# The transposed copy in a blocked triangular inverse moves from VectorE to TensorE and ScalarE

## The reference

```python
def step(s, inp):
    rt, wt, kt, vt, kkt, bt = inp
    sa = jnp.einsum('bhvk,bhk->bhv', s, kkt)
    s = s * wt[:, :, None, :] - sa[..., None] * bt[:, :, None, :] + vt[..., None] * kt[:, :, None, :]
    return s, jnp.einsum('bhvk,bhk->bhv', s, rt)
```

## Time and profile before

| | |
|---|---|
| median of 3 runs | 3190.02 us (3181.11 to 3193.24) |
| the profiled execution, its time | 3199.97 us |
| its span, first to last instruction | 3198.4 us |
| TensorE busy, matmul | 2887.4 us, 90% |
| VectorE busy | 1812.4 us, 57% |
| ScalarE busy | 1227.5 us, 38% |
| GpSimd busy | 520.2 us, 16% |
| mean granted TensorE clock | 0.951 |
| recurrence of layer 0, first mask to last "done" | 465.01 to 624.28 us |

### The profile page before, as it was taken

The page is one execution under the profiler, slowest core; times in us unless marked ns, Lnnn a source line. Parts: engine busy times, 40 slices in busy tenths (PEclk is TensorE's granted clock), DMA queues, the critical chain, the costliest instruction groups (busy, mean ns, idle before and its releaser), DMA issues. The chain is left out here.

```text
span 3198.4 us, 64194 instructions
## 1 busy us (share of the span) xinstructions
PE 2887.4 (90%) x25830; PEld 2672.7 (84%) x25830; DVE 1812.4 (57%) x2810; ACT 1227.5 (38%) x1637; POOL 520.2 (16%) x341
## 2 busy tenths in 40 slices
PE   7998988889988899899989988987899889998997
PEld 7997877677687898799989978876777878987997
DVE  4444757676666564544344348576765765654442
ACT  4534521044332443444245355210543234434442
POOL 0003640044320000000000046401543100000000
PEclk9999999899999999999989999998999989999998
DMA  4444340144283556344344443401443744663442
GB/s 159 151 143 135 124 126 4 32 122 165 88 307 106 191 205 223 125 144 145 119 140 147 144 133 113 123 4 32 129 172 99 282 161 162 218 216 121 149 147 100
DMA packets 119697, 448.22 MB, mean 140 GB/s; under 512 B 13648, under 2 KB 23920, under 8 KB 111664
## 3 DMA queue, kind: packets, MB, share of 16 engines
q1 hardware_dynamic: 97920, 329.75, 31.4%
q0 software_dynamic: 21552, 115.34, 9.9%
HBM read 397.01 MB, written 48.02 MB: 139 GB/s over the span
## 5 line engine op out<-in xcount | busy, mean ns | idle before, releaser
L1542 ACT ACTIVATE w_high<-ring 128x1024 fp32r<-128x1024 f32 x598 | 632.0, 1057 | 788.6 <-PE gemm_banks L886 331.8
L882 PE MATMUL gemm_banks<-in_high,w_high 128*128 128x320 f32 (+1 forms) x2736 | 810.2, 312 | 24.0 <-DVEq L2263 12.2
L1938 DVE TENSOR_TENSOR w_low<-ring,w_high 128x1024 fp32r<-128x1024 f32 x436 | 532.5, 1222 | 493.5 <-ACT w_high L1542 492.9
L883 PE MATMUL gemm_banks<-in_low,w_high 128*128 128x320 f32 (+1 forms) x2736 | 799.5, 308 | 0.0
L720 POOL TENSOR_TENSOR w_low<-ring,w_high 128x1024 fp32r<-128x1024 f32 x162 | 411.8, 2547 | 927.8 <-ACT w_high L1542 924.0
L882 PEld LDWEIGHTS gemm_banks<-in_high,w_high 128*128 128x128 f32 x2736 | 517.6, 189 | 31.5 <-DVEq L2263 13.2
L883 PEld LDWEIGHTS gemm_banks<-in_low,w_high 128*128 128x128 f32 x2736 | 517.5, 189 | 2.7
L886 PE MATMUL gemm_banks<-in_high,w_low 128*128 128x320 f32 (+1 forms) x2736 | 452.7, 308 | 6.0 <-POOL w_low L720 3.8
L886 PEld LDWEIGHTS gemm_banks<-in_high,w_low 128*128 128x128 f32 x2736 | 410.4, 188 | 8.5 <-POOL w_low L720 4.9
L939 PE MATMUL gemm_banks<-in_high,w_high 128*128 128x320 f32 x640 | 208.1, 338 | 23.4 <-DVE arena L2037 20.2
L966 PE MATMUL gemm_banks<-act_high,w_high 128*128 128x320 f32 x704 | 215.1, 319 | 3.3 <-DVE arena L1987 3.3
(11 more groups left out here) (427 smaller groups left out, 4344.5 us busy)
## 6 DMA issues: line engine op xcount, KB each, us to landing
ring<-in_w SPq DMA_DIRECT2D x598, 512.0 KB, 3.5
arena<-in_kc POOLq DMA_DIRECT2D x14, 1024.0 KB, 6.4
arena<-in_vc POOLq DMA_DIRECT2D x14, 1024.0 KB, 8.1
out_fill<-stage SPq DMA_DIRECT2D x80, 160.0 KB, 3.9
arena<-in_ssm POOLq DMA_DIRECT2D x16, 512.0 KB, 13.4
out_s_ssm<-arena POOLq DMA_DIRECT2D x16, 512.0 KB, 14.4
arena<-in_ret POOLq DMA_DIRECT2D x16, 512.0 KB, 22.3
out_s_ret<-arena POOLq DMA_DIRECT2D x16, 512.0 KB, 7.8
```

The lines of the kernel that those rows point to most:

```text
L882: mm(dst, w_high[:, slot, w(k)], in_high[:, k, 0:n], start=(k == 0), stop=False)
L883: mm(dst, w_high[:, slot, w(k)], in_low[:, k, 0:n], start=False, stop=False)
L1542: f(w_high[:, slot], ring[:, s, 0:D], ACT.Copy).then_inc(weights_high, 1)
L1938: tt(w_low[:, slot], ring[:, pos % RING, 0:D], w_high[:, slot].bitcast(F32), ALU.subtract).then_inc(weights_split, 1)
```

## The change

XT is kept with the two heads of a pair exchanged: the partitions of one head hold the transpose of the other. So is Y.

- VectorE no longer makes or updates XT: L2131 and L2139 (both groups) and L2162 (both groups, levels 1 to 4; level 1 in the sample chunk) are gone. Btok moves into `start_x`, ahead of the addition that sets the mark "masked". The masks of RBc, RKc and LkTc are spread over levels 1 to 3 and no longer 2 to 4.
- In level 1 TensorE transposes X into bank 2 with the identity as moving operand, `crossed`, 8 matmuls for a group.
- ux becomes `crossed`, so that Y comes out exchanged.
- xy has, below the last level, first `heads` with the identity as weights, which puts the old XT into PSUM, then the product for X, now `crossed` and to bank 3, then the update of XT, which adds to the same PSUM region. In the last level only the product for X is left.
- ScalarE copies XT from bank 2 to SBUF for each level and group, mark ("xt", m - 1); xy(m, g) waits for it. It comes before the early copies in ScalarE's list.
- "g" of `early` goes to bank 0 and no longer to the second half of bank 3, and ux of level 5 no longer waits for the copy of it.

```diff
--- before.py
+++ after.py
@@ -256,6 +256,8 @@
         if c == NCH:
             add("read", "P")
             add("reads", "V")
+        for m in levels_of(c):
+            add(("xt", m - 1), "A")
         add("early", "A")
         if c == NCH:
             add("cross", "P")
@@ -1109,7 +1111,7 @@
                     def early(g, p, q, steps):
                         for step in steps:
                             if step == "g":
-                                ins_ = crossed(view(g, 3, 256)[:, q], LkTc[:, p], Vc[:, p])
+                                ins_ = crossed(view(g, 0, 0)[:, q], LkTc[:, p], Vc[:, p])
                             if step == "y":
                                 ins_ = crossed(view(g, 1, 0)[:, q], Vc[:, p], RKc[:, p])
                             if step == "state":
@@ -1119,21 +1121,26 @@
                         for g in GROUPS:
                             if m == 1:
                                 need(A, (c, "tokens", g))
-                            if (m, g) == (5, 0):
-                                need(A, (c, "early", 0))
                             need(V, (c, "masked", g) if m == 1 else (c, ("x", m - 1), g))
-                            each_pair(g, ("ux", m), lambda p, q: heads(view(g, 3, 0)[:, q], Lc[:, p], Xc[:, p]))
+
+                            def ux(p, q):
+                                if m == 1:
+                                    crossed(view(g, 2, 0)[:, q], Xc[:, p], i2)
+                                return crossed(view(g, 3, 0)[:, q], Lc[:, p], Xc[:, p])
+                            each_pair(g, ("ux", m), ux)
                         for g in GROUPS:
+                            need(A, (c, ("xt", m - 1), g))
                             need(V, (c, ("y", m), g))
 
                             def xy(p, q):
-                                ins_ = heads(view(g, 2, 0)[:, q], XTc[:, p], Yc[:, p])
-                                if (m, g) == (4, 0):
+                                if (m, g) in ((4, 0), (5, 1)):
                                     early(g, p, q, ("g", "y"))
-                                if (m, g) == (5, 1):
-                                    ins_ = early(g, p, q, ("g", "y"))
+                                xt = view(g, 2, 0)[:, q]
                                 if m < levels_of(c)[-1]:
-                                    ins_ = heads(view(g, 2, 256)[:, q], Yc[:, p], XTc[:, p])
+                                    heads(xt, i2, XTc[:, p], stop=False)
+                                ins_ = crossed(view(g, 3, 256)[:, q], XTc[:, p], Yc[:, p])
+                                if m < levels_of(c)[-1]:
+                                    ins_ = heads(xt, Yc[:, p], XTc[:, p], start=False)
                                 return ins_
                             each_pair(g, ("xy", m), xy)
                     if c == NCH:
@@ -1719,16 +1726,21 @@
                         else:
                             A_(f(Ktokbd[0:64, gs, 64:128], kt[0:64], ACT.Copy))
                             A_.mark(f(Ktokbd[64:128, gs, 0:64], kt[64:128], ACT.Copy), A, (c, "tokens", g))
+                    for m in levels_of(c):
+                        for g in GROUPS:
+                            need(M, (c, ("xy", m - 1) if m > 1 else ("ux", 1), g))
+                            xt = bank(4 * g + 2)[:, 0:256].rearrange("p (a b) -> p a b", b=64)
+                            A_.mark(f(XTc[:, 4 * g:4 * g + 4], xt, ACT.Copy), A, (c, ("xt", m - 1), g))
                     for g in GROUPS:
                         gs = slice(4 * g, 4 * g + 4)
-                        b3, b1 = (bank(4 * g + k)[:, a:a + 256].rearrange("p (a b) -> p a b", b=64) for k, a in ((3, 256), (1, 0)))
+                        b0, b1 = (bank(4 * g + k)[:, 0:256].rearrange("p (a b) -> p a b", b=64) for k in (0, 1))
                         if c < NCH:
                             need(M, (c, ("xy", 4 + g), g))
-                            A_(f(Gc[:, gs], b3, ACT.Copy))
+                            A_(f(Gc[:, gs], b0, ACT.Copy))
                             A_.mark(f(Bt[:, gs, tc], b1, ACT.Copy), A, (c, "early", g))
                         else:
                             need(M, (c, "cross", g))
-                            A_.mark(f(Gc[:, gs], b3, ACT.Copy), A, (c, "early", g))
+                            A_.mark(f(Gc[:, gs], b0, ACT.Copy), A, (c, "early", g))
                     for g in GROUPS:
                         need(M, (c, "solve", g))
                         sa = bank(4 * g + 2)[:, 0:256].rearrange("p (a b) -> p a b", b=64)
@@ -2124,11 +2136,6 @@
                         need(M, (c, "products", g))
                         V_(tt(Xc[:, gs], bv(g, 0, 0, 128)[:, :, 0:64], rep(K("nm0"), 4), ALU.mult))
                         V_(tt(Lc[:, gs], bv(g, 2, 0), rep(K(pre + "lo"), 4), ALU.mult))
-                        V_.mark(tt(Xc[:, gs], Xc[:, gs], rep(K("ident2"), 4), ALU.add), V, (c, "masked", g))
-
-                    def start_xt(g):
-                        gs = slice(4 * g, 4 * g + 4)
-                        V_(tt(XTc[:, gs], bv(g, 2, 0), rep(K("nm0t"), 4), ALU.mult))
                         bt = bv(g, 2, 256)
                         if c < NCH:
                             V_(ts(Btok[:, gs], bt, -1.0, None, ALU.mult))
@@ -2136,7 +2143,7 @@
                             for hh in range(2):
                                 r_ = head_rows(hh)
                                 V_(ts(Btokbd[r_, gs, r_], bt[r_], -1.0, None, ALU.mult))
-                        V_(tt(XTc[:, gs], XTc[:, gs], rep(K("ident2"), 4), ALU.add))
+                        V_.mark(tt(Xc[:, gs], Xc[:, gs], rep(K("ident2"), 4), ALU.add), V, (c, "masked", g))
 
                     def mask_rb(g):
                         gs = slice(4 * g, 4 * g + 4)
@@ -2158,35 +2165,31 @@
                     def x(m, g):
                         gs = slice(4 * g, 4 * g + 4)
                         need(M, (c, ("xy", m), g))
-                        if m < lv[-1]:
-                            V_(tt(XTc[:, gs], XTc[:, gs], bv(g, 2, 256), ALU.add))
-                        V_.mark(tt(Xc[:, gs], Xc[:, gs], bv(g, 2, 0), ALU.add), V, (c, ("x", m), g))
+                        V_.mark(tt(Xc[:, gs], Xc[:, gs], bv(g, 3, 256), ALU.add), V, (c, ("x", m), g))
 
                     start_x(0)
-                    start_xt(0)
                     start_x(1)
                     y(1, 0)
-                    start_xt(1)
+                    mask_rb(0)
                     y(1, 1)
+                    mask_rk(0)
                     x(1, 0)
                     x(1, 1)
                     y(2, 0)
-                    mask_rb(0)
+                    mask_lk(0)
                     y(2, 1)
-                    mask_rk(0)
+                    mask_rb(1)
                     x(2, 0)
                     x(2, 1)
                     if c < NCH:
                         y(3, 0)
-                        mask_lk(0)
+                        mask_rk(1)
                         y(3, 1)
-                        mask_rb(1)
+                        mask_lk(1)
                         x(3, 0)
                         x(3, 1)
                         y(4, 0)
-                        mask_rk(1)
                         y(4, 1)
-                        mask_lk(1)
                         x(4, 0)
                         x(4, 1)
                         y(5, 0)
```

## The result

The changed kernel is slower: 3205.53 us, median of 9 runs (3200.13 to 3211.05), beside 3189.32 us for the kernel before (median of 9, 3180.53 to 3193.24). The ratio is 1.0051, 95% interval 1.0036 to 1.0065. The forecast was 3175, so it missed by 30 us and in sign. The profiled execution of the changed kernel took 3209.05 us (span 3207.4 us).

The account below looks back on a forecast made before the run. VectorE was taken to bound levels 2 to 4, a VectorE-TensorE chain level 5. Gain 17.4 us less 2.4 for waits made 15.0, so the median 3190.02 becomes 3175; range 3164 to 3188.

Parts of the forecast that it names:

- level 5 to x(5,1): Last level, y(5,0) to x(5,1): 2.97 us for 2.58 before, a loss of 0.39 a chunk.
- What TensorE gets: TensorE's part in the recurrence: the 24-matmul xy priced at 0.93 us if heads and crossed mix, 1.39 if not.
- The double wait: Each xy waits for two semaphores: 0 to 0.06 us each, 0 to 4.8 in all, 2.4 taken.
- 2.17: Net gain in us of each prompt chunk, summed over its levels; 17.4 over 2 layers of 4 chunks.
- Heads and crossed mix at 0.93: In xy, both kinds of matmul run side by side, so the diagonal sets the time: 0.93 us.
- ScalarE's copy hides: XT copy per level and group, over 0.49 us after xy(m-1), covered by 1.8 us of other work: cost nothing.
- The sample chunk gained nothing: Ninth part: TensorE's reads wait for the state load, so losing 6 VectorE instructions gains 0.
- The falls of the clock to half: Level 1 in five of eight chunks: 4.2 us more gained if they vanish, 4.3 less if they stay; 0 taken.
- The 0.20 us between a possible next group and a last result: TensorE timing: a group's last result comes about 0.20 us after the next group could start.
- TensorE does not mix: Rival: identity and update add 0.46 us to each xy, 2.0 lost a chunk, total 3209; chance 0.09.
- a spacing of 1.39: Sign in levels: 1.39 us between the xy groups, instead of 0.93, makes the forecast wrong at once.
- ScalarE's copies: Sign in TensorE's timeline: gaps that end with ScalarE's copies make the forecast wrong at once.

Follow-up runs that it names:

- e9_half_early: Changed kernel with each group's identity product as two matmuls of 256 columns, placed between the waits for ScalarE's copy and for Y; 3180.86 us, ratio 0.9974 to before.
- e5: Changed kernel with the wait for Y moved behind the first identity pair, except in the last level; 3194.80 us, ratio 1.0025 to before.
- after_again: The changed kernel profiled once more, nothing altered; 3195.52 us in its one run.
- e3: Changed kernel with each group's identity product as two matmuls of 256 columns, not eight of 64; 3182.72 us, ratio 0.9995 to before.
- e1: Kernel before with eight unused crossed products added to each xy below the last level in the prompt chunks; 3199.93 us, ratio 1.0042 to before.
- e7: e1 with a second, long satisfied wait ahead of each xy; 3208.50 us, ratio 1.0068 to before.
- e8: Kernel before with only a second, already satisfied wait ahead of each xy, no matmul added; 3196.14 us, ratio 1.0015 to before.
- e6: Changed kernel with twenty tiny matmuls of 8 columns (the pad, 80 instructions) ahead of each layer's first chunk; 3221.82 us in its one run.

## Why the prediction was wrong

The forecast laid chunk 1 out in parts. Set against the profiles (y(2,0) counted from the chunk's first mask, then y to y, the tail from x(5,1)):

| part | forecast | after | e9_half_early |
|---|---|---|---|
| start and level 1 | 7.24 | 8.49 | 7.91 |
| level 2 | 3.11 | 4.77 | 3.11 |
| level 3 | 3.11 | 4.81 | 3.11 |
| level 4 | 3.57 | 5.50 | 3.52 |
| level 5 to x(5,1) | 2.97 | 3.12 | 3.10 |
| tail | 8.24 | 8.03 | 8.45 |

- **The step that failed** is in "What TensorE gets": the xy was priced at 0.93 us by the quarters of the array alone. Against the array that is right, 504.31 to 505.24. But a matmul was taken to cost only its time on the array. 16 more matmuls a level are 64 more instructions, and with TensorE now in the chain their supply showed: gaps of 0.74 to 1.64 us in this chunk, each at the border of a block of 256 instructions. The levels came to 4.77, 4.81 and 5.50 us for 3.11, 3.11 and 3.57.
- **The double wait** was given 0 to 0.06 us for each xy, half of 4.8 in all. Its own time was sized rightly: a level without a gap takes 3.21 us in the changed kernel and 3.11 in e5, 0.05 for each xy. But removing it below the last level (e5) gave back 1.6 to 1.9 us a chunk, 13 to 15 us in all. The bound was the gap that an idle engine needs to start again. It did not ask what TensorE could have done ahead of time.
- **The two together** are the miss. By the forecast the mean chunk is 30.86 - 2.17 + 0.30 (its 2.4 us for the waits) = 29.0 us. After and after_again have 32.5, so 3.5 us a chunk and 28 us in all are missing, of the 30 between the medians (3175 and 3205.5). From there e5 takes 1.8, and the shorter list of e9 the other 1.9, down to 28.84. That these are stalls of instruction supply is shown by the packet ahead of each gap, by the one place modulo 256 at which they all end, by the move with the pad, and by e3. That the second wait costs by making a block come later against TensorE's place is shown by the lead in e1 and e7, before and e8. Why the request comes later is argued: the sequencer stops at that wait, and the queue's request seems to follow the sequencer; no row ties the two.
- **The mechanisms that held.** VectorE lost its 12 instructions and the bound passed to TensorE. Heads and crossed mix at 0.93. ScalarE's copy hides: xy(2,0) at 504.31 was released by L2163 of VectorE and not by a copy. The sample chunk gained nothing (36.4 us for 36.1); GpSimd's load was issued at 595.10, and TensorE's reads began at 608.82, released by it. The falls of the clock to half did get fewer, from five in the eight prompt chunks to two (534.4 and 2073.8). The forecast took nothing for them. Its price of 0.85 us each was near the 0.7 to 0.8 of the rows above, and in e3, e5 and e9 they vanish altogether, which is 4 us of e9's gain over the first profile of before. Beside 30 us they are small.
- **Smaller misses.** Even in e9, with the levels at 3.11, the start and level 1 took 7.91 us for 7.24, of which 0.44 is one more gap at the border of a block (499.76), and level 5 took 3.10 for 2.97. The 0.20 us between a possible next group and a last result is 0.17 in the rows it was read from (1.10 less 0.93).
- **The rivals.** "TensorE does not mix" gave 3209, near the measured time, but for a reason that the profile refutes: its sign would have been a spacing of 1.39. The text named that and ScalarE's copies as what would make it wrong, and neither happened. Every rival priced the array, the clock or VectorE. None asked whether the engine gets its instructions in time.
- **What was there to see.** The kernel before already had "issue" waits of 2.2 us from 463 to 590, one of 0.95 us at 528.08 at the start of a chunk, and the queue of instructions stood on its page with 158 packets. They were harmless as long as VectorE was the bound.

The Trainium skill ("Runtime: NRT & Kernel Launch", Instruction fetch mechanics) says that instructions arrive in blocks of 16 KiB, 256 instructions. The packets of the queue and the count agree. It also says that the fetch is hidden, because a sequencer dispatches more slowly than the blocks come in. Here the trace disagrees: gaps of up to 1.9 us stand behind the packets (e6, 484.83), at the border of the block, in levels that would use 256 instructions in 3.2 us.

Open are some 7 of the timed 10 us of e1, which its two profiles do not place, the 5 to 7 us between e9's profile and its medians, and what sets the moment at which a packet is requested.

## What to carry to other kernels

When work is moved to TensorE as many small fp32 matmuls, count instructions as well as columns: each is four, and a stretch that uses 256 of them in 3 to 4 us with TensorE in the chain can be paced by their supply (here a block came 2.2 to 2.9 us after its request). Make fewer and wider ones of the same form (64 rows by 256 columns kept the quarters apart; the full 128x128 form did not pay), and give each instruction one wait, with independent work put between two. Look for "issue" gaps before the change: an engine that is off the critical path hides them, and they come out when it becomes the bound. If the gaps stand at places 256 instructions apart, it is supply.

## What the runs showed of the hardware

- 64x64 fp32 matmuls on the two diagonals mix freely: 24 matmuls on quarters took 0.93 us, 16 of them on one diagonal; at 256 columns they mix as well (e3: xy to xy 501.04 to 501.95, 0.91).
- TensorE's instructions came in packets of 16 KB, 256 at a time (56 packets for 8 chunks of 1797, 66 for 8 of 2126). All 176 "issue" gaps over 0.3 us ended at one place modulo 256 in their layer, 2.18 to 2.93 us after a packet started.
- A second wait that is always satisfied cost 0.5 to 0.8 us a chunk of 30.6 us at 192 TensorE instructions a level and 1.6 to 1.9 at 256 (about 0.9 and 1.6 to 1.8 without the falls of the clock, an estimate). A chunk has ten such xy.
- TensorE's place in its blocks of 256 instructions matters: 80 instructions ahead of the loop changed single chunks by up to 5.2 us (layer 1, 37.13 to 31.91; in layer 0, 30.87 to 35.68).
- A fall of the granted clock to 0.50, 3.4 us long, in the start or level 1 of a chunk cost 0.7 to 0.8 us of the kernel before (9.35 to 9.43 for 8.62).
- One 128x128 fp32 matmul with 256 columns held the array for 0.63 us, where the two 64x64 ones with 256 columns of e3 took 0.45 us (501.04 to 501.49) and left the other diagonal free.
